# Reordering VectorE's queue inside the seven-product blocks of a two-layer decoder step

## What is computed

```python
def squared_relu_mlp(x, w1, w2):
    return jnp.square(jax.nn.relu(x @ w1)) @ w2

def trunk(...):
    for layer in range(DEPTH):
        ...
        x = layer_norm(DEEPNORM_ALPHA * x + mix, ln1_g[layer], ln1_b[layer])
        x = layer_norm(DEEPNORM_ALPHA * x + squared_relu_mlp(x, mlp_w1[layer], mlp_w2[layer]), ln2_g[layer], ln2_b[layer])
```

## Time and profile before

| | us |
|---|---|
| median of 3 runs | 2427.0 (2426.45 to 2431.1) |
| the profiled execution | 2428.9 |
| its span, first to last instruction | 2427.0 |
| PE busy | 2335.8 |
| VectorE busy | 1301.7 |
| GpSimd busy | 633.2 |

### The profile page before, as it was taken

One profiled execution on the slowest core, in us unless ns is written; L12 is line 12 of the kernel. 1 busy time (PEld: TensorE's weight loads), 2 busy tenths in 40 slices (PEclk: granted clock), 3 DMA queues, 4 the chain that ended last, 5 costly groups with the idle time before them and its releaser, 6 DMA issues.

```text
span 2427.0 us, 35451 instructions
## 1 busy us (share of the span) xinstructions
PE 2335.8 (96%) x13822; PEld 2073.3 (85%) x13822; DVE 1301.7 (54%) x2312; ACT 640.9 (26%) x1260; POOL 633.2 (26%) x282
## 2 busy tenths in 40 slices
PE   8999999999999999999999899999999999999997
PEld 7988878898998998998999666688898898898896
DVE  3556566547437437355733756456645626626547
ACT  1223204211221211223300366505121221221223
POOL 2101212124324234223521100112133324324320
PEclk9999999999999999999999999999999999999999
DMA  5201231232322321322322467642232232232232
GB/s 176 63 26 36 89 99 57 83 105 73 109 89 71 116 89 62 124 85 73 120 67 70 172 237 276 257 48 70 70 122 92 80 103 92 80 103 90 83 97 99
DMA packets 69735, 245.95 MB, mean 101 GB/s; under 512 B 25584, under 2 KB 30320, under 8 KB 61040
## 3 DMA queue, kind: packets, MB, share of 16 engines
q1 hardware_dynamic: 52944, 173.68, 21.0%
q10 hardware_dynamic: 16688, 70.83, 9.7%
HBM read 230.33 MB, written 81.97 MB: 129 GB/s over the span
## 4 chain that ended last, share of the span: by engine, by line
PE 43%; issue 27%; POOL 14%; DVE 7%; DMA 5%; ACT 2%; SPq 1%; POOLq 0%; DVEq 0%; ACTq 0%
PE PS L1750 20%; PE PS L1826 13%; POOL WS L626 12%; DMA RAW<-in_zb 3%; PE PS L2027 2%; POOL RAW L664 1%; PE PS L2155 1%; PE PS L2129 1%; DMA WR<-in_w 1%; PE PS L1772 1%; PE PS L2194 1%; PE PS L2168 1%; DVE XT L1142 1%; PE PS L2143 1%; PE PS L1871 1%
## 5 line engine op out<-in xcount | busy, mean ns | idle before, releaser
L1750 PE MATMUL PS<-XS,WS 128*128 128x384 f32 (+1 forms) x7056 | 1191.6, 328 | 16.8 <-DVE XS L1058 11.0
L1750 PEld LDWEIGHTS PS<-XS,WS 128*128 128x128 f32 x7056 | 1165.8, 189 | 33.8 <-issue 20.7
L626 POOL TENSOR_TENSOR WS<-RAW,WS 128x1024 fp32r<-128x1024 f32 x140 | 344.6, 2462 | 723.3 <-DVE WS L1449 644.8
L2027 PE MATMUL PS<-WS,AR 128*128 128x512 f32 x2016 | 466.8, 390 | 15.4 <-DVE XT L1433 15.4
L2027 PEld LDWEIGHTS PS<-WS,AR 128*128 128x128 f32 x2016 | 377.0, 188 | 97.9 <-DVE XT L1433 20.4
L617 POOL TENSOR_TENSOR WS<-WR,WS 128x1024 fp32r<-128x1024 f32 x74 | 185.3, 2504 | 834.4 <-DVE WS L1068 834.4
L1420 DVE TENSOR_TENSOR AR<-HR,AR 128x1024 fp32r<-128x1024 f32 x84 | 116.3, 1385 | 422.5 <-ACT AR L871 422.5
L1433 DVE TENSOR_TENSOR XT<-XT,PS 128x512 f32<-128x512 f32 x360 | 233.2, 679 | 47.2 <-PE PS L2027 44.9
L878 ACT ACTIVATE RT<-PS 128x384 f32<-128x384 f32 (+1 forms) x144 | 68.2, 474 | 612.8 <-PE PS L1750 612.8
L1826 PE MATMUL PS<-WS,XS 128*128 128x512 f32 x768 | 179.9, 394 | 4.1 <-DVE XT L1289 4.1
L1826 PE MATMUL PS<-WS,HID 128*128 128x512 f32 x768 | 177.3, 390 | 0.0
(11 more groups left out here) (224 smaller groups left out, 1814.2 us busy)
## 6 DMA issues: line engine op xcount, KB each, us to landing
WR<-in_w SPq DMA_DIRECT2D x74, 512.0 KB, 3.7
out_d_ks<-in_cache_d_k ACTq DMA_DIRECT2D x96, 340.0 KB
out_d_vs<-in_cache_d_v ACTq DMA_DIRECT2D x96, 340.0 KB
RAW<-in_zw SPq DMA_DIRECT2D x56, 512.0 KB, 3.2
RAW<-in_zb SPq DMA_DIRECT2D x48, 512.0 KB, 5.5
KC<-in_kt SPq DMA_DIRECT2D x16, 1024.0 KB, 10.7
VCD<-in_cache_d_v SPq DMA_DIRECT2D x16, 1024.0 KB, 7.1
TG<-in_rows SPq DMA_DIRECT2D x10, 512.0 KB, 5.6
```

What stands on the lines that cost most here:

```text
L626: pool.tensor_tensor(WS[:, slot, 1, :], RAW[:, r, :], WS[:, slot, 0, :].bitcast(F32), ALU.subtract).then_inc(z_split, 1)
L1750: last = pe.matmul(out[:, 0:gw], WS[:, slot, a, (off + k) * P:(off + k + 1) * P], src[:, b, k, c0:c0 + gw], start=(n == 0), stop=(n == 3 * ...
L2027: last = pe.matmul(bank(Z_BANKS[op][e]), AR[:, op % 2, a, k, e * P:e * P + P], WS[:, z_slot(Z_OPERAND[op]), f, 512 * k:512 * k + 512], sta ...
```

## The change

Only the order of VectorE's instructions in `strassen` changes; two `taken_in` calls of four and of four banks are split in two, and two others are joined. The instructions are the same and as many. Nothing changes on the other engines' queues.

- The pack moves ahead of operand 3.
- The low part of product 3 moves ahead of the second sum; the first quarter of product 2 is taken in between the second and the third sum; the other three quarters follow the third sum.
- The low part of product 4 moves ahead of operand 6, and product 2's quarters with it.
- All four quarters of product 3 are taken in at once behind operand 6, and the fourth sum moves behind them.
- Operand 7 moves behind the low part of product 5, operand 8 behind that of product 6; operand 9 goes between two halves of product 5's quarters.

```diff
                 dve.tensor_tensor(RAW[:, 1, :], RAW[:, 4, :], RAW[:, 1, :], ALU.subtract).then_inc(z_late, 1)
-                operand(3, z_slot(2), 1, unit=11, late=2)
                 dve.wait_ge(zh_sq, 12 * i + (12 * N_Z * l + 12))
                 dve.tensor_tensor(KT[:, :, :], HR[:, 0:2, SEQ:NT], HR[:, 2:4, SEQ:NT], ALU.add)
...
                 dve.tensor_tensor(PKZ[:, 4:6, 1, :], KT[:, :, :], PKZ[:, 4:6, 0, :].bitcast(F32), ALU.subtract).then_inc(z_packed, 1)
+                operand(3, z_slot(2), 1, unit=11, late=2)
                 taken_in(1, d4[0:2], Z_BANKS[0][0:2], ALU.add)
                 total(1, a21, a21, a22, ALU.add)
                 operand(4, z_slot(3), 2, unit=12)
...
                 taken_in(6, d1, Z_BANKS[1], ALU.add)
+                low(3, a21)
                 total(2, a11, a21, a11, ALU.subtract)
+                taken_in(10, d4[0:1], Z_BANKS[2][0:1], ALU.subtract)
                 total(3, a12, a12, a11, ALU.subtract)
-                low(3, a21)
+                taken_in(11, d4[1:4], Z_BANKS[2][1:4], ALU.subtract)
+                low(4, a12)
                 operand(6, z_slot(1), 0, product=Z_FREE[1])
-                taken_in(10, d4, Z_BANKS[2], ALU.subtract)
-                low(4, a12)
+                taken_in(14, d3, Z_BANKS[3], ALU.add)
                 dve.wait_ge(a_ready, 7 * i + (7 * N_Z * l + 3))
                 total(4, a22, a22, a11, ALU.subtract)
-                taken_in(14, d3[0:2], Z_BANKS[3][0:2], ALU.add)
-                operand(7, z_slot(2), 4, product=Z_FREE[2])
-                taken_in(16, d3[2:4], Z_BANKS[3][2:4], ALU.add)
                 taken_in(18, d4[0:1], Z_BANKS[4][0:1], ALU.add)
                 low(5, a22)
-                operand(8, z_slot(3), 1, product=Z_FREE[3], nth=2)
+                operand(7, z_slot(2), 4, product=Z_FREE[2])
                 taken_in(19, d4[1:4], Z_BANKS[4][1:4], ALU.add)
                 low(6, a11)
+                operand(8, z_slot(3), 1, product=Z_FREE[3], nth=2)
                 taken_in(22, [XT[:, N_TILES - 1, 512:1024]], (7,), ALU.add)
+                taken_in(23, d2[0:2], Z_BANKS[5][0:2], ALU.subtract)
                 operand(9, z_slot(0), 2, product=Z_FREE[4], nth=2)
-                taken_in(23, d2, Z_BANKS[5], ALU.subtract)
+                taken_in(25, d2[2:4], Z_BANKS[5][2:4], ALU.subtract)
```

## The result

| | before | after |
|---|---|---|
| median of runs, us | 2429.05 (4 runs, 2426.45 to 2432.59) | 2397.89 (4 runs, 2396.20 to 2399.82) |
| ratio, 95% interval | | 0.9871 (0.9854 to 0.9888) |
| the profiled execution, its span | 2428.9, 2427.0 | 2398.41, 2396.5 |

The changed kernel is 1.3% faster. The two spans lie 30.5 us apart, the medians 31.2.

A forecast was written before the change was run, and what follows sets the result against it. PE, busy 96% of the span, bounds the kernel; only ending its waits for VectorE helps. 2.56 us a block x 12 is 30.7 at most, 29.9 by idle times; 30 taken from 2428.9 gives 2399, median 2397; range 2393 to 2408.

The forecast's parts named there:

- The sum: Over the twelve seven-product blocks, ending PE's two waits gives 30 us, between 29.9 and 30.7; median 2397.
- the upper way, by starts: PE's loss in the stage counted from matmul starts: 2.56 us a block x 12, 30.7 us at most.
- The way by idle times: PE's listed 23.4 us idle plus 24 breaks at 0.27 for lost overlap and first matmul: 29.9 us.
- The pack: Placed where operand 3 stood, its first cast takes 0.29 us; 2.2 us to spare, 0.84 + 0.14 a block go.
- Rival two: The pack's first cast takes 2.50 us by itself; only 5.4 us gained, 2421.6; chance 0.03.
- The way to product 3: VectorE's new order up to product 3's two quarters leaves 0.6 and 0.2 us to spare; 1.44 + 0.14 a block go.
- Behind it: VectorE's work after product 3's second quarter stays in time, 1.8 us to spare for product 5's low part; no cost.
- A new wait at product 3's second quarter: PE waits there if the chain, tight by 0.2 us, comes later; 2400 to 2410; chance 0.10.
- The wait that moves without a reason: Chain 2.5 us late at product 3's second quarter, no row showing why; stall as before, 2427; chance 0.03.
- rival three: VectorE's two-input instructions get ahead of fills 3, 4 and 5, each then 4.37 us; 44 us more, 2471; chance 0.03.

The follow-up runs named there:

- the spare place: To the changed kernel, one more VectorE addition of 768 elements a block behind the low part of product 4, ahead of operand 6; median 2398.2 us.

## Why the prediction was right

**The sum.** Foretold 30 us between the bounds 29.9 and 30.7; the stages give 30.6, so the upper way, by starts, was the exact one. The way by idle times falls short because the first few matmuls behind a break also start a few thousandths of a microsecond further apart, some 0.02 to 0.03 in all. The median foretold, 2397, lies 0.9 below the one measured; that it came so near is in part luck, since the executions spread by 3.6 us (changed) and 6.1 us (before), and the differences outside the stage cancel.

**The pack.** The open price was the cast alone, between 0.23 and 0.69, taken as 0.29: it is 0.284 to 0.288 in all twelve blocks. Rival two (slow by itself) is out: the pack's return behind the fill brought 2.50 back. This agrees with what the Trainium skill, "SBUF — State Buffer", section "Who interferes with whom", says of the pair of ports that VectorE and GpSimd share: the instruction that issues first keeps it for its whole length. The sum ahead of the fill shows it in both directions (1.22 and 3.32 instead of 2.46 and 2.41). The other instruction is not held quite to the end: a sum that comes second ends 1.08 us behind the fill, and alone it takes 1.22.

**The way to product 3.** Every step of the chain came within 0.03 us of its foretold distance from product 0's start: the low part of product 3 ends 15.75 behind it (foretold 661.14 - 645.41 = 15.73), the first add 17.49 (17.47), the second 19.22 (19.21). The spare times 0.64 and 0.27 at the two quarters were foretold as 0.6 and 0.2. Three kernels confirm that they are real: 0.6 us more in the queue ahead of the second add costs 0.47 a block, 0.87 costs 0.75, and one sum ahead of the first add costs 0.75.

**Behind it.** The spare 1.8 us for product 5's low part showed when 0.87 were taken from it and nothing came. That operands 9 and 10 would be held by fills stood in no sentence of the prediction, which counted on held two-input instructions alone behind the pack. It cost nothing: operand 9's fill ends at 679.36, 3.3 us ahead of the units that need it (682.65), where 4 or more was foretold.

**The rivals.** A new wait at product 3's second quarter did not come, but the place was right: it is where the wait goes when a cast or an addition is put ahead of the second add (one sum ahead of the first add brings it back at the first quarter). The wait that moves without a reason (four) is out with it. Of rival three, a fill coming second was made once and had no cost, against a mechanism that needs it three times; the time of 2471 for that case was not tried. Its price was wrong: the 4.37 of the earlier trace rows belongs to an instruction of twice the width, and the fill took 3.32, about where the prediction itself says that this rival begins to decide. It also left out that the sum which comes first is done 1.24 us sooner (1.22 instead of 2.46), so that the chain was 0.2 us earlier and not later.

**What each part is worth.** The pack alone takes 1.15 us off the stage (44.26 to 43.11), all but the pack 1.47 (to 42.79), the whole 2.52. The parts add up to a little more than the whole (2.62), since the pack alone also shortens product 3's wait, from 1.28 to 1.08, which the rest would end anyway; the 0.11 of the run of 96 works the other way.

## What to carry to other kernels

When one engine bounds the time and another feeds it from a hand-ordered queue, write down the due time of each thing fed and follow the queue forward from durations in the trace: the least spare time tells where a wait will appear, and what may be moved for nothing. Look at long outliers of short instructions on VectorE: if GpSimd runs at that moment, another place in the order can make them short (2.50 to 0.28 us here), and an instruction that reads from PSUM is the right one to put behind whatever starts GpSimd (0.67 to 0.69 us in all 360 cases, fills or not). Idle time in a list of waits understates a break on PE (0.18 us listed cost 0.47); starts of matmuls give the loss.

## What the runs showed of the hardware that was not expected

Kernels with the same stages differ by some microseconds outside of them, and the clock has a part in it. The kernels with the added instruction at the spare place and with the first sum ahead of the fill both have stages of 41.74 us, yet their spans are 2392.5 and 2396.7. In both, PE waits 2.5 us for VectorE ahead of a run of transposes at about 134 us. Stretches of the two (length, busy time of PE, PEld, DVE, ACT, POOL, granted clock, DMA share), the spare place first:

```profile
134.00:137.50 3.50, 3.50 (x25) 2.96 (x24) 1.66 (x8) 1.02 (x1) 0.00 (x0) 1.00 0.30 117
308.00:311.50 3.50, 3.50 (x18) 2.88 (x17) 0.04 (x1) 0.00 (x0) 0.00 (x0) 1.00 0.90 14
```

The first sum ahead of the fill:

```profile
134.00:137.50 3.50, 3.50 (x17) 2.34 (x16) 0.33 (x1) 1.02 (x1) 0.00 (x0) 0.54 0.29 117
308.00:311.50 3.50, 3.50 (x11) 2.72 (x10) 1.73 (x2) 0.00 (x0) 0.00 (x0) 0.55 0.82 175
```

In one the granted clock stays at 2.4 GHz, in the other it is at 1.2 GHz for nearly the whole stretch, in code that neither edit touches; the second block starts at 635.95 in the one and at 640.98 in the other. Ahead of layer 1's attention the half clock lasted longer in the changed kernel than before: over 10 us at 0.50, where the low stretch before was 3.5 us long.

```profile
1353.00:1363.00 10.00, 8.63 (x21) 3.98 (x21) 4.31 (x11) 2.76 (x6) 0.00 (x0) 0.50 0.98 378
```

PE had waited 3.0 us for VectorE just ahead of it, and had done so in the kernel before too. Why the clock falls in one run and stays in another was not tried. A change that is worth less than such stretches has to be read from the stage, not from the time.
